# A hybrid decoder trunk: branch C's probability rows are turned by VectorE in 32 by 32 squares instead of by TensorE

## The reference, cut to what matters

```python
DEPTH, D_MODEL, BLK, N_META = 2, 1024, 128, 16
def hybrid_layer(x, ...):                       # twice
    h = split_cols(x @ w_in)
    out_a = causal_dense_attention(qa, ka, va, key_valid, HEAD_DIM ** -0.5, decay)
    out_b = mla_attention(...)
    out_c = dsa_sparse_attention(q, k, v, iq, ik, iw, ...)
    out_d = sliding_window_sink_attention(...)
    mixed = concat([out_a * silu(a_g), out_b * silu(b_g), out_c * silu(c_g), out_d * silu(d_g)])
    y = mixed @ w_out
    return layer_norm(ALPHA * x + y, ln_g, ln_b)
# branch C, one block of 128 queries, 8 heads of 64 that share 2 key/value heads:
    score = einsum(relu(iq . ik), iw);  _, idx = top_k(score, 256)
    logits = q . k[idx] * d ** -0.5 + rel_bias_c[bucket(distance)]
    probs = softmax(where(allowed, logits, NEG));  out = probs @ v[idx]
```

## Time and profile before

| | |
|---|---|
| median of 3 runs | 3281.66 us (3280.83 to 3294.05) |
| the profiled execution | 3284.43 us |
| its span | 3282.6 us |
| mean granted TensorE clock | 0.978 of 2.4 GHz |
| busy: PE, DVE, ACT, POOL | 93%, 51%, 31%, 17% |

### The profile page before, as it was taken

How to read it: one execution, slowest core, us unless ns; L and a number is a source line. 1 busy time by engine, 2 the same in 40 slices (tenths; PEclk the granted TensorE clock), 3 DMA queues, 4 the chain that set the end, 5 groups by cost and what they waited for, 6 DMA issues and landing times. The chain is left out here.

```text
span 3282.6 us, 39947 instructions
## 1 busy us (share of the span) xinstructions
PE 3037.5 (93%) x14214; PEld 1741.1 (53%) x14214; DVE 1690.1 (51%) x4523; ACT 1017.9 (31%) x2749; POOL 566.8 (17%) x994
## 2 busy tenths in 40 slices
PE   6899999999898999989998999998998889999999
PEld 4345666555455565544453456665554556565443
DVE  4225877766666534421122278777766654444122
ACT  1223333334344333310012233343344443333000
POOL 1001222111111123310000012221111111333000
PEclk8999999999999999999999999999999999999999
DMA  5101110111000012042211011101010000200321
GB/s 201 47 26 33 40 41 30 38 35 44 15 20 15 14 30 100 15 142 62 77 61 35 13 35 46 41 30 41 25 51 14 15 16 23 95 30 22 117 76 56
DMA packets 91004, 153.05 MB, mean 47 GB/s; under 512 B 12656, under 2 KB 68224, under 8 KB 88504
## 3 DMA queue, kind: packets, MB, share of 16 engines
q1 hardware_dynamic: 90808, 150.50, 13.9%
HBM read 120.36 MB, written 32.21 MB: 46 GB/s over the span
## 5 line engine op out<-in xcount | busy, mean ns | idle before, releaser
L967 PE MATMUL ps_s<-xT,w_ring 128*128 128x348 f32 (+2 forms) x3616 | 1133.5, 467 | 4.3 <-DVE gate L1386 2.6
L967 PEld LDWEIGHTS ps_s<-xT,w_ring 128*128 128x128 f32 x3616 | 673.7, 191 | 395.8 <-issue 99.0
L1548 POOL TENSOR_SCALAR arena<-arena,small 128x256 f32<-128x256 f32 (+9 forms) x576 | 361.6, 639 | 1603.5 <-DVE small L1461 1602.3
L1196 ACT ACTIVATE arena<-arena,small 128x256 f32<-128x256 f32 (+9 forms) x576 | 380.2, 660 | 195.4 <-DVE small L1449 195.1
L1207 ACT ACTIVATE arena<-ps_t 128x512 f32<-128x512 f32 (+4 forms) x700 | 308.8, 471 | 374.6 <-PE ps_t L1034 365.7
L1034 PE MATMUL ps_t<-ident,arena 128*128 128x128 f32 (+2 forms) x2432 | 356.6, 274 | 50.4 <-ACT arena L1207 34.9
L1237 DVE MAX8 small<-score 128x8 f32<-128x1040 f32 (+6 forms) x448 | 376.3, 840 | 10.5
L1239 DVE MATCH_REPLACE8 score<-small,score 128x1040 f32<-128x1040 f32 (+6 forms) x448 | 369.9, 826 | 0.0
L1034 PEld LDWEIGHTS ps_t<-ident,arena 128*128 128x128 f32 (+2 forms) x2432 | 253.3, 131 | 209.6 <-issue 96.3
L1046 PE MATMUL ps_o<-arena 128*64 128x256 f32 (+3 forms) x2816 | 316.6, 362 | 20.7 <-ACT cT L1130 12.3
L1011 PE MATMUL ps_s<-feat 64*128 64x256 f32 (+12 forms) x1888 | 307.9, 428 | 28.8 <-DVE small L1449 24.1
(11 more groups left out here) (147 smaller groups left out, 2347.1 us busy)
## 6 DMA issues: line engine op xcount, KB each, us to landing
w_ring<-in_w_feat SPq DMA_DIRECT2D x78, 512.0 KB, 3.5
mixed<-mixg SPq DMA_DIRECT2D x128, 128.0 KB, 1.7
feat<-mixed SPq DMA_DIRECT2D x16, 1024.0 KB, 6.7
resid<-score SPq DMA_DIRECT2D x16, 512.0 KB, 3.1
score<-resid SPq DMA_DIRECT2D x16, 512.0 KB, 7.5
arena<-in_w_out SPq DMA_DIRECT2D x4, 1536.0 KB, 8.1
cT<-falls SPq DMA_DIRECT2D x8, 520.0 KB, 4.8
feat<-falls SPq DMA_DIRECT2D x8, 520.0 KB, 5.3
```

The lines of the kernel that those rows point to most:

```text
L967: mm = pe.matmul(ps_s[:, bank, 0:w], w_ring[:, wt % 2, k, :], xT[:, k, c0:c0 + w], start=(k == 0), stop=(k == KT - 1))
L1196: nc.scalar.activation(p, p, ACT.Exp, scale=-1.0, bias=nm[:, e:e + 1], accum_out=psums[0:M, st % 4, e:e + 1]).then_inc(S["exp_done"], 1)
L1548: nc.gpsimd.tensor_scalar(p, p, rinv[0:M, st % 4, e:e + 1], 1.0, ALU.mult, ALU.mult).then_inc(S["nrm_done"], 1)
```

## The change

In branch C alone:

- TensorE's transposes, the copies out of `ps_t` and the products into `ps_o` are gone. VectorE transposes a block's row in place, every square of 32 by 32 for itself (`tr`), two blocks later. So partition quarter r then holds, for each block of 32 keys, those keys on its partitions and the 32 queries of quarter r on its columns. Rows keep a place of their own in SBUF until they are used (`c_row`), the last 16 columns of the last square are zeroed by GpSimd (in `near`).
- The values are multiplied per group of blocks (`pvc`): blocks 5 to 8 after block 2, blocks 0 to 4 at block 6 of the next pair. For each block of 32 keys there are eight products: four row quarters (32 partitions each, into four banks, 4 to 7) and two column halves (one per head). The values lie in SBUF once per quarter, in blocks of 32 keys (`v_sub`), brought there by way of memory (`values`, stored at `iw`, read back at `vr`).
- VectorE reads four banks per group for the gate (`gtc`).
- `G` moves to blocks 8, 5, 4, `Q` to blocks 7, 3, 1. The mixed rows of block 8 are loaded at block 1 instead of 3 of the last pair. `w_out` goes elsewhere in SBUF: six of 16 pieces are loaded at the second pair (`w0`), seven after the first group of the last pair (`w1`), three at the end (`wo`).

The diff, cut to its core:

```diff
-W_OUT_SETS = [4, 3, 3, 3, 3]
+W_OUT_SETS = [3, 3, 4, 3, 3]
+TURNED = {1: (range(5, NB), 0, 1984, 1056), 2: (range(0, 5), 8064, 960, 544)}
+SUB = 32
...
+    def pair_c(self, l, p):
...
+        for idx, work in zip((0, 3, 4), self.tile(l, "G", br="C", p=p)):
...
+            for idx, work in zip((1, 5, 7), self.tile(l, "Q", br="C", p=p + 1)):
...
+            put(7, lambda: self.add("yl", l=l, b=ORDER[0], yy=yy, ln=None))
+            put(8, lambda: self.y_parts.pop(0)())
...
+            if len(self.turn_next) == 2:
+                self.add("tr", **self.turn_next.pop(0))
...
+            if (idx == 2 and p) or idx == 6:
+                self.turned_values(l, p if idx == 6 else p - 1, 1 if idx == 6 else 2, P_BANK)
...
+            if idx == 6 and p == NP - 1:
+                self.add("w1", l=l)
...
+                elif kind == "vr":
+                    sp.wait_ge(S["vs_st"], 32 * (l + 1))
+                    sp.wait_ge(S["pv_done"], 2 * it["upto"]["pv"])
+                    for j in range(4):
+                        src = bass.AP(values[l], 0, [[2 * HD, SUB], [SUB * 2 * HD, 32], [1, 2 * HD]])
+                        sp.dma_start(v_sub[SUB * j:SUB * (j + 1), 0:32, :], src).then_inc(S["vr_ld"], 16)
...
+                elif kind == "pvc":
+                    pe.wait_ge(S["tr_done"], it["turned"])
...
+                    for b in range(-(-keys_of(last) // SUB)):
+                        rows = min(SUB, keys_of(last) - SUB * b)
+                        lo = min(i for i in blocks if keys_of(i) > SUB * b)
+                        for e in range(2):
+                            for r in range(4):
...
+                                mm = pe.matmul(psum[HD * e:HD * (e + 1), bank + r, c0:c1],
+                                               v_sub[part, b, HD * e:HD * (e + 1)], turned,
+                                               start=(b == 0), stop=True, skip_group_check=True)
+                    mm.then_inc(S["pv_done"], 2)
...
+                elif kind == "tr":
+                    st, i, n, M = it["st"], it["i"], it["n"], it["M"]
+                    dve.wait_ge(S["pad_done"], it["nb"] + 1)
+                    for e in range(2):
+                        dve.wait_ge(S["nrm_done"], 2 * st + 1 + e)
+                        row = p_row(it, e, 0, n + SUB - N_META)
+                        dve.transpose(row, row).then_inc(S["tr_done"], 1)
+                elif kind == "gtc":
...
+                    for r in range(4):
+                        t = dve.scalar_tensor_tensor(to[:, :, r], done[:, :, r], 0.5, by[:, :, r], ALU.mult, ALU.mult)
```

More of the change, by code:

```diff
@@ L82, in buffer_of, with c_row @@
     return "Z" if a == 0 else ("X" if a % 2 == 0 else "Y")
+def c_row(i):
+    blocks, at, step, share = TURNED[1 if i >= 5 else 2]
+    return at + step * (i - blocks[0]), share
 def key_cols(br, i, kb):
@@ new lines, in turned_values, with flush_c @@
+    def turned_values(self, l, p, group, bank):
+        pv = self.take("pv")
+        self.c_used[group] = 2 * (pv + 1)
+        it = dict(l=l, br="C", p=p, group=group, pv=pv, bank=bank,
+                  turned=self.last_turn[group],
+                  waits=self.banks([bank] if bank else [0, 1, 2, 3], ("o_free", pv + 1)))
+        self.add("pvc", **it)
+        self.gt_next = it
+    def flush_c(self, l):
+        more = self.y_parts
+        more.pop(0)()
+        self.normalise()
+        for s in self.turn_next:
+            self.add("tr", **s)
+            more.pop(0)()
+        self.turn_next = []
+        self.turned_values(l, NP - 1, 2, 0)
+        self.gated()
@@ L478, in build @@
     turned = [nc.dram_tensor(f"turned{l}", (ROPE, NTOK), F32, kind="Internal") for l in range(DEPTH)]
+    values = [nc.dram_tensor(f"values{l}", (NTOK, 2 * HD), F32, kind="Internal") for l in range(DEPTH)]
     lines = nc.dram_tensor("lines", (2 * NH, LINE), F32, kind="Internal")
@@ L521, in build @@
         vw = sb("vw", [BLK, KT * 384])
-        w_out += [vw[:, k * D_MODEL:(k + 1) * D_MODEL] for k in range(3)]
+        w_out = [vw[:, k * D_MODEL:(k + 1) * D_MODEL] for k in range(3)]
         u_q = vw[:, 0:2048].rearrange("p (k c) -> p k c", k=2)
@@ L534, in build @@
         x_new = score[:, 2048:4096].rearrange("p (r n) -> p r n", r=2)
-        x_in = ([arena[:, nVC + k * D_MODEL:nVC + (k + 1) * D_MODEL] for k in range(4)]
+        x_in = (wide(nVC, 3) + wide(gR + 4 * D_MODEL, 1)
                 + [feat[:, k, 0:D_MODEL] for k in (0, 2, 3)] + [res_in[:, k] for k in range(2)])
@@ L673, in p_row @@
         def p_row(it, e, c0, w):
+            if it["br"] == "C":
+                at, share = c_row(it["i"])
+                at += gR + e * share + c0
+                return arena[0:it["M"], at:at + w]
             at = ROW_AT[it["row"]]
@@ L1525, in _ @@
                         pool.wait_ge(near_ld[it["hu"] % 2], 32 * (it["hu"] // 2 + 1))
+                    waits(pool, it["rwaits"])
+                    at, share = c_row(i)
+                    pads = arena[0:M, gR + at:gR + at + 2 * share].rearrange("p (e k) -> p e k", e=2)
+                    nc.gpsimd.memset(pads[:, :, n:n + SUB - N_META], 0.0).then_inc(S["pad_done"], 1)
+                    if it["idx"] == 0:
                         if p == 0:
```

195 lines of the change are left out of this document (134 added, 61 removed).

## The result

| | before | changed |
|---|---|---|
| median of 20 runs | 3284.28 us | 3309.93 us |
| lowest to highest | 3271.31 to 3294.74 | 3289.32 to 3317.22 |
| ratio | | 1.0065, interval 1.0051 to 1.0080 |
| profiled execution, its span | 3284.43, 3282.6 us | 3297.06, 3295.3 us |
| mean granted clock | 0.978 | 0.966 |

A forecast was written before the change was run, and what follows sets the result against it. TensorE, busy 93% of the span, was taken to bound the kernel; six pairs at -82 us and last pairs at +12 gave -70 from 3284.4: 3214, or 3212 as median. Its own range was 3188 to 3235, the full range 3185 to 3285.

The forecast's parts named there:

- 9.6 us for the values: TensorE's new products per pair of branch C: 8.9 us with all eight side by side, plus 0.7 for narrow blocks.
- rival 2: TensorE cannot be fed 1600 value instructions a pair; decides from 11 ns each; sums of 3490 or 3850 us; chance 0.08.
- The clock: TensorE's speed: a fall charged only after the last pair's hole, about 3 us more for the output projection.
- the hole of the last pair: TensorE idles 15 us before the first output matmul, as the mixed rows' load queues behind w_out.
- The 0.7 us for the sixteen narrow blocks: Addition to each pair's values, as 32 or 64 columns are too short to cover the next weights.
- The base of a pair: A pair's terms beside its values: projections 29.3 us, scores 11.2, overlap -1.5, waits 3.2; with values 52 us.
- rival 3: The chain of VectorE, ScalarE and GpSimd sets branch C's pace; 58 us a pair, 3248 us; chance 0.13.
- The last pair: Branch C's fourth pair per layer: 78 us to the 14th output matmul against 72, loss 6, twice: +12 us.
- the wait for w_out behind it: A second TensorE gap in the last pair, 4 to 5 us, for the last 1.5 MB of w_out.
- the walk: Block-by-block sum of the last pair: 39.5 + 16 + 7 + 3 + 3.2 + 9.4 = 78 us.
- the transposes: VectorE's 18 in-place transposes a pair, 12.8 us, hidden under projections; VectorE then at 30.7 of 52 us.
- Rival 1: Only four of eight value products run together (+69 us), or a 24 ns start floor (+77); chance 0.15.

The follow-up runs named there:

- few_instructions: Changed kernel with last-pair rows loaded before w_out, second-group values ahead of output projection, and narrow key blocks multiplied for both heads at once: 0.9890 to before, 3248.49 us.
- first_block_only: The changed kernel with only the products of the first key block issued in each group's values: 0.9712 to the kernel before.
- rows_first: The changed kernel with seven pieces of w_out issued behind the load of the mixed rows in C's last pair: 1.0040 to the kernel before.
- halves_inner: The changed kernel with row quarter as outer loop and column half (head) as inner loop of the values' products: 1.0081 to the kernel before.

## Why the prediction was wrong

1. **The feed**, the step "9.6 us for the values", failed: its columns were nearly right (eight side by side; the starts inside the runs add up to 10.2 us), but the 1600 instructions were priced only in rival 2. That rival named the mechanism and its point ("from 11 ns per instruction (18 us a pair)"); the chip gives 13.5 ns behind the first lots, and the pair has 17.9 us. I gave it 0.08 because no row showed a limit; the densest row, at 55 ns, could not show one, and I let silence count as evidence. Price: 6.4 us a pair of gaps and 1.4 of drawn ends before them, 7.8 of the 12.6 us of the miss. (Rival 2's own prices stood on guesses of 28 and 55 ns; the last one adds up to some 3840, not 3850.)
2. **The clock.** The sum held TensorE at full speed in the pairs, since before it was 1.00 there. I charged a fall behind the hole of the last pair (3 us) and not behind the new waits of the pairs: 3.2 us in the second.
3. **Narrow products.** The 0.7 us for the sixteen narrow blocks was too little: at 32 and 64 columns a record takes 10 ns in the bursts, where the rate by columns gives 3.6 and 7. The whole streaming term is short by 0.6 us, 10.2 for 9.6.
4. **The base of a pair** was nearly right as long as the values cover VectorE. In few_instructions the pair less its values (13.54 us and 2.5 of gaps) is 43.2 us, where my terms give 42.2. With nearly no values it was not: first_block_only has 51.0 us, of it 1.0 of values, and TensorE waits for VectorE's chain (rival 3). With values of 9.6 us a pair would take 52.8 by the first of these, an estimate if no covered wait comes to light; which holds at 9.6 us was not measured.
5. **The last pair.** Right: the hole (15 forecast, 15.82 measured) and its cause (rows_first). Too large: the wait for w_out behind it, 1.71 and 3.08 us for "4 to 5". The last pairs lost 22.5 us for 12, and their values took some 21 us more than the walk had for them (three groups in each: 23.4 and 23.0 us for 12.8); what gave the rest back was not taken apart.
6. **Right:** the transposes (1.2 us for 1056 columns, 1.25 measured; VectorE 29.6 us for 30.7), and that they are hidden, but for the first pairs and the 1.69 us wait in the last ones.
7. **Rival 1** with its floor, which I tied to a rule, gave nearly the right time for a wrong reason: the sums agree (19 us of values) because 24 ns is near 2 x 13.5. The bursts show starts 10 to 15 ns apart for hundreds of records, so neither 24 nor 25 ns is a floor for such products. The time alone would have confirmed it, and that would have been luck.

Over all, the six pairs gave -6.7 us in place of -82 and the last ones +22.5 in place of +12: 86 of the 98 us between forecast and median. The other 12 are for the most part the profiled execution's distance from its median (13 us), and no trace shows them.

## What to carry to other kernels

Count instructions as well as columns: cutting products into small tiles that fill the array multiplies weight loads and passes, and a stretch of some hundreds of them can be paced by their delivery. A gap on TensorE costs itself and often a slower clock behind it; so close the gaps first, and use wide products where the array has room. Splitting a long run in pieces did not help here. Before an engine's work is moved off the path, look at what it covers.

## What the chip showed that I had not expected

- Instructions of TensorE arrive in lots of 256 (16 KB); behind the first 214 to 484 one lot took 3.45 us or a little more, with 0.9 to 1.3 us of it the packet itself.
- Eight products of 32 rows and 64 columns run side by side, eight records of 128 columns in 109 ns; of 32 rows and 128 columns four do, in 432 ns for 256 columns. The order of the two halves made no difference (halves_inner).
- The 32 by 32 transpose of 1056 f32 columns takes 1.25 us.
- A wait of 2.25 us on TensorE was followed by a projection of 7.34 us in place of 4.9; one of 2.33 us in the same pair was not (4.87 us).
